# Conv means ahead of the first rotation, and the attention's modulation pair as direct TensorE products

## The chip, the cores and the metric

The program runs on one core of one Trainium2 chip. The metric is the device time of one launch, in microseconds (us); lower is better. The core has a matrix engine (TensorE, "PE" in the profile), a vector engine (VectorE, "DVE"), an engine for functions and copies (ScalarE, "ACT"), GpSimd ("POOL") and SyncE ("SP"), which here only issues DMA transfers. Each engine works through its own instructions in order; they wait for each other on semaphores. TensorE's clock has two levels here, 2.4 GHz (a granted clock of 1.00) and 1.2 GHz (0.50).

## The reference, cut to what matters

Two blocks are computed one after the other, three layers in all. The change is in the first layer, of this function:

```python
for l in range(DEPTH):
    sh1, sc1, g1, sh2, sc2, g2 = adaln(c, w_mod[l], b_mod[l])            # silu(c) @ w_mod + b_mod, split in 6
    csh1, csc1, cg1, csh2, csc2, cg2 = adaln(c_ctx, w_mod[l], b_mod[l])
    h = modulate(rms_norm(x, norm1_g[l]), sh1, sc1)
    hc = modulate(rms_norm(xc, norm1_g[l]), csh1, csc1)
    q, k, v, up, ca, cb = project_inputs(h, w_in[l], q_norm_g[l], k_norm_g[l])
    qc, kc, vc, upc, cac, cbc = project_inputs(hc, w_in[l], q_norm_g[l], k_norm_g[l])
    q = apply_rope(q, cos, sin)
    k = apply_rope(k, cos, sin)
    attn = diff_attn_post(diff_attention(q, k_all, v_all, lam), subln_g[l], lambda_init)
    pool_o = pool_mixer(up, pool_w[l], pool_scale[l])
    conv_o = conformer_conv(ca, cb, ...)       # depthwise conv of 31 taps, layer_norm over 256 channels, silu
    mix = jnp.concatenate([attn, pool_o, conv_o], axis=-1)
    x = x + g1 * jnp.einsum('blm,md->bld', mix, w_out[l])
...
```

The model has 1024 channels, 512 tokens and 256 context tokens; four heads, each with two score maps of 64 channels.

## The kernel before, in words

Tokens lie in the free dimension (512 + 256 in layer 0, `TOK` = 768), channels on the 128 partitions. Weights come in blocks of 256 columns. SP loads a block into `raw`, ACT copies it to a rounded high part (`w_hi`), GpSimd subtracts to get the low part (`w_lo`), and PE multiplies three times (high by high, high by low, low by high). In layer 0's input blocks 2 to 9 DVE makes the low part itself (`own_lo`), since GpSimd computes the pool windows there.

Layer 0 has ten input blocks. Blocks 0 to 3 give the inputs of convolution and pool, 4 to 7 give queries and keys (two tiles of 128 channels each), 8 and 9 give the values. Four output blocks follow the attention. Everything is written out by hand, engine by engine; no scheduler moves anything.

**Modulation pairs.** The columns of `w_mod` are taken 512 at a time, as a "pair" (l, p) of two rings of 256. SP loads a pair once the pair before it is saved (`load_pair`, semaphores `mod_saved` and `mod_landed`). DVE multiplies each of the eight row tiles by the condition's column and adds up, 16 steps for condition and context condition together (`pair_steps`, L2174, over `mod_w` and `mod_ctx`). PE then sums over the partitions by eight matmuls with a column of ones (`pair_sum`, L2494; in the trace a float32 matmul leaves two records, so 16), and DVE or ACT copies eight columns to `modc`. Pair (0,7), `PAIR_ATT`, has its 16 steps in two halves behind rotations 2 and 3, its sums in `second_root`, its copy on ACT (L2042); the first scores wait for that. Pair (0,6) belongs to block 7, pair (0,8) to the first output block.

**The queries and keys.** For tile pair j (blocks 4 to 7) ACT squares and copies, PE sums the squares by head (`head_sum`, L2634), ACT takes the root, DVE inverts it (`inverse`). For the rotation SP swaps odd and even channels by DMA (`load_swap`, semaphore `p_swap`); `rotate(j)` is three DVE instructions (L2263 to L2265). The swap of j = 2 and 3 waits until rotation j - 2 is done. For keys the root is spread by ACT (`spread_root`), turned by PE (`turn_root`, L2706) and multiplied in by DVE (`finish_k`, L2273).

**The convolution.** 62 taps on DVE leave `conv_acc`. PE sums over the channels (`conv_sums`, L2666, behind the first tile of block 7), DVE subtracts the mean (L2305, `c_yc`), ACT squares, PE sums again (`conv_square_sum`, L2686), ACT and DVE make the root (`c_root`), ACT spreads it, PE turns it (`conv_root_turned`, L691, behind tile 4 of block 8) and DVE multiplies (L2327, `c_yn`). In block 7 `head_sum` of keys waits for `c_yc`.

**GpSimd.** The pool windows start when the last step of pair (0,6) is done.

**The attention.** 24 units in layer 0, six to a head: four of 128 queries by 768 keys, then two small ones of 128 context queries by 256 context keys. PE makes the scores of unit u + 2, multiplies by v for unit u - 1 where a pair of units is complete, and turns unit u (`later`). PE's order between blocks 8, 9 and the attention is set by these dictionaries:

```python
between = {4: conv_root_turned} if b == 8 else {
    0: lambda: turn_root(4), 2: second_root, 3: first_score, 4: lambda: turn_root(6),
    5: lambda: turn_root(7)}
```

## Time and profile before

| | |
|---|---|
| three runs | 2577.93, 2583.73, 2584.11 us; median 2583.73 |
| the profiled execution | 2577.28 us, of which 2575.5 us from its first to its last instruction |
| busy shares | PE 95%, PE's weight loads 78%, DVE 52%, ACT 31%, POOL 34% |
| mean granted TensorE clock | 0.966 |
| chain that ended last | PE 86%, DVE 9%, ACT 3%, issue 1%, DMA 1% |
| DMA | 240.57 MB, mean 93 GB/s |

The chain follows the work that ended last back to its start, each step to what released it. A row of the timeline gives start and length of merged instructions of one line; in brackets stands how long the engine was idle before, and who ended that. Pages and rows are of one execution. Busy PE is not PE at its peak: at a clock of 0.50 it is busy twice as long for the same work.

### The profile page before, as it was taken

The page shows a single profiled execution, that of the slowest core. Times are in us where ns is not written, and L with a number is a line of the kernel's source. Part 1 is how long each engine was busy: PE and PEld are TensorE (multiplying, and loading weights), DVE is VectorE, ACT ScalarE, POOL GpSimd, SP SyncE. Part 2 cuts the span into 40 slices and gives each one's busy share as a digit, 9 for nine tenths or more (in the row PEclk, how much of TensorE's full clock was granted, in tenths as well). Part 3 has the DMA queues.
Part 4 walks back from the last instruction along what each step waited for, and adds up shares of the span by engine and source line. Part 5 has one row for each costly group of instructions (what it writes and reads, how often), then busy time and mean ns, then how long its engine had stood idle before and what let it go on. Part 6 is the DMA issues. An engine that isn't in the chain of part 4 may idle for free.

```text
span 2575.5 us, 30755 instructions
## 1 busy us (share of the span) xinstructions
PE 2445.3 (95%) x13017; PEld 2019.1 (78%) x13017; DVE 1337.2 (52%) x1709; ACT 798.5 (31%) x1088; POOL 884.9 (34%) x633
## 2 busy tenths in 40 slices
PE   7999899999999999899999999998999988999998
PEld 3888778788888888778777778877988557888886
DVE  2899766646444343695656655654562424211113
ACT  2222661311211111425732122235343443222222
POOL 2006002223333332365034445543453003454442
PEclk9898899899999999899999999998999999999999
DMA  8332203224334242232034546432113002233331
GB/s 265 95 104 83 66 1 111 70 87 143 99 113 132 82 131 82 65 107 75 1 98 131 149 146 175 151 115 66 50 35 114 17 1 65 70 95 98 90 98 58
DMA packets 309225, 240.57 MB, mean 93 GB/s; under 512 B 10692, under 2 KB 304831, under 8 KB 309087
## 3 DMA queue, kind: packets, MB, share of 16 engines
q1 hardware_dynamic: 308674, 238.47, 30.5%
q8 instruction: 103, 1.69, 0.3%
q14 instruction: 34, 0.28, 0.0%
q10 hardware_dynamic: 414, 0.13, 0.0%
HBM read 232.29 MB, written 2.10 MB: 91 GB/s over the span
## 4 chain that ended last, share of the span: by engine, by line
PE 86%; DVE 9%; ACT 3%; issue 1%; DMA 1%; POOL 0%; SPq 0%; DVEq 0%; ACTq 0%
PE ps L2542 62%; PE ps L1162 5%; DVE mod_w L2174 2%; PE ps L2577 2%; PE ps L946 2%; PE ps L684 2%; DVE mod_ctx L2174 1%; PE ps L733 1%; PE ps L1182 1%; PE ps L2457 1%; PE ps L2494 1%; PE ps L760 1%; DVE small L1050 1%; PE ps L908 1%; ACT probs L990 1%
## 5 line engine op out<-in xcount | busy, mean ns | idle before, releaser
L1680 POOL TENSOR_TENSOR w_lo<-raw,w_hi 128x512 fp32r<-128x512 f32 x518 | 757.2, 1492 | 1380.5 <-ACT w_hi L1788 1380.4
L2542 PE MATMUL ps<-h_hi,w_hi 128*128 128x512 f32 x1994 | 649.4, 372 | 25.2 <-DVE h_lo L2138 21.1
L2542 PE MATMUL ps<-h_lo,w_hi 128*128 128x512 f32 x1994 | 639.5, 367 | 0.0
L2542 PE MATMUL ps<-h_hi,w_lo 128*128 128x512 f32 x1994 | 638.9, 366 | 0.0
L1788 ACT ACTIVATE w_hi<-raw 128x2048 fp32r<-128x2048 f32 (+2 forms) x155 | 264.8, 1708 | 577.3 <-PE ps L2542 365.3
L2542 PEld LDWEIGHTS ps<-h_hi,w_hi 128*128 128x128 f32 x1994 | 340.4, 191 | 93.9 <-issue 23.1
L2542 PEld LDWEIGHTS ps<-h_hi,w_lo 128*128 128x128 f32 x1994 | 339.9, 190 | 67.1
L2542 PEld LDWEIGHTS ps<-h_lo,w_hi 128*128 128x128 f32 x1994 | 340.4, 190 | 65.9 <-issue 0.2
L2065 ACT ACTIVATE xg<-ps 128x512 f32<-128x512 f32 (+1 forms) x66 | 44.2, 670 | 679.4 <-PE ps L2542 492.6
L2174 DVE SCALAR_TENSOR_TENSOR mod_w<-mod_w,cond 128x512 f32<-128x512 f32 x224 | 242.0, 1080 | 3.4
L2542 PE MATMUL ps<-hid_hi,w_hi 128*128 128x512 f32 x704 | 231.7, 370 | 0.0
L2542 PE MATMUL ps<-hid_lo,w_hi 128*128 128x512 f32 x704 | 230.3, 368 | 0.0
L2542 PE MATMUL ps<-hid_hi,w_lo 128*128 128x512 f32 x704 | 230.3, 368 | 0.0
L2423 DVE TENSOR_TENSOR sq<-xg,ps 128x512 f32<-128x512 f32 (+1 forms) x66 | 51.1, 775 | 342.6 <-ACT xg L2065 342.5
L2201 DVE SCALAR_TENSOR_TENSOR x<-ps,modc,x 128x512 f32<-128x512 f32 (+1 forms) x160 | 100.6, 678 | 208.1 <-PE ps L2542 208.1
L2542 PEld LDWEIGHTS ps<-hid_hi,w_lo 128*128 128x128 f32 x704 | 120.4, 188 | 24.6
L2542 PEld LDWEIGHTS ps<-hid_lo,w_hi 128*128 128x128 f32 x704 | 120.5, 188 | 24.3
L2542 PEld LDWEIGHTS ps<-hid_hi,w_hi 128*128 128x128 f32 x704 | 120.5, 188 | 24.0
L2426 DVE TENSOR_TENSOR hid_lo<-sq,hid_hi 128x512 fp32r<-128x512 f32 (+1 forms) x66 | 90.2, 1367 | 85.8 <-ACT hid_hi L2068 85.8
L1087 DVE SCALAR_TENSOR_TENSOR conv_acc<-u_conv,col_b,conv_acc 128x783 f32<-128x783 f32 (+1 forms) x120 | 123.6, 1030 | 4.2
L2174 DVE SCALAR_TENSOR_TENSOR mod_ctx<-mod_w,cond,mod_ctx 128x512 f32<-128x512 f32 x112 | 108.3, 967 | 0.0
L1162 PE MATMUL ps<-h_hi,w_hi 128*128 128x512 f32 (+1 forms) x196 | 73.3, 374 | 0.9 <-POOL w_lo L1680 0.9
(380 smaller groups left out, 3225.8 us busy)
## 6 DMA issues: line engine op xcount, KB each, us to landing
mod_w<-in_w_mod SPq DMA_DIRECT2D x72, 1024.0 KB, 9.6
raw<-in_w_ffn_in SPq DMA_DIRECT2D x88, 512.0 KB, 5.3
raw<-in_w_in SPq DMA_DIRECT2D x54, 512.0 KB, 4.9
raw<-in_w_ffn_out SPq DMA_DIRECT2D x48, 384.0 KB, 3.8
raw<-in_w_out SPq DMA_DIRECT2D x24, 512.0 KB, 4.6
raw<-in_w_gate SPq DMA_DIRECT2D x22, 512.0 KB, 4.0
raw<-in_w_up SPq DMA_DIRECT2D x22, 512.0 KB, 5.4
raw<-in_w_down SPq DMA_DIRECT2D x24, 384.0 KB, 3.8
```

The source lines that it names most:

```text
L684: ins = pe.matmul(ps[:, at + j:at + j + 1], square[:, P * j:P * j + P], ones[:, 0:1], start=first and j == 0, stop=last, skip_group_check= ...
L946: ins = pe.matmul(ps[:, PV2_AT:PV2_AT + 256], values(us[u]["k0"] // P + k, us[u]["h"]), probs_t[:, k, 256 * (j % 2):256 * (j % 2) + 256], ...
L1087: ins = dve.scalar_tensor_tensor(acc, frm, w, acc, ALU.mult, ALU.add)
L1162: ins = pe.matmul(ps[:, at:at + tw], weight, v[:, k, t0:t0 + tw], start=(k == 0 and r == 0), stop=(k == KD - 1 and r == 2))
L1680: ins = pool.tensor_tensor(w_lo[:, s, at:end], raw[:, s, at:end], w_hi[:, s, at:end].bitcast(F32), ALU.subtract)
L1788: act.activation(w_hi[:, s, 0:floats], raw[:, s, 0:floats], ACT.Copy).then_inc(hi_ready, 1)
L2174: ins = dve.scalar_tensor_tensor(to, w, by, to if step >= chains else mod_bias[:, :, :], ALU.mult, ALU.add)
L2201: ins = dve.scalar_tensor_tensor(xt, ps[:, at:at + tw], modc[:, l % 2, chunk + 2 * b + t, c:c + 1], xt, ALU.mult, ALU.add)
L2423: dve.tensor_tensor(ffn_h[:, s, 0:T], ffn_sg[:, s, 0:T], ps[:, 2048 * s + 1024:2048 * s + 1024 + T], ALU.mult).then_inc(psum_free[s], 1)
L2426: dve.tensor_tensor(hid_lo[:, i, 0:T], ffn_h[:, s, 0:T], hid_hi[:, i, 0:T].bitcast(F32), ALU.subtract).then_inc(f_lo, 1)
L2542: ins = pe.matmul(ps[0:m, at:at + tw], weight(part, k, cols), v[:, held[k] if held else k, t0:t0 + tw], start=(at_k == 0 and j == 0 and no ...
L2577: ins = pe.matmul(ps[:, first + width * t:first + width * (t + 1)], v[:, k, rows], w[:, k, :], start=(k == 0 and j == 0), stop=(k == KD - ...
```

## The change

It has four parts, all in layer 0.

1. DVE subtracts the conv means after 4 steps of pair (0,6), ahead of rotation 0, where it had done 8 steps and rotation 0 first. The other 12 steps follow, then the low part of block 8, rotation 0, the low part of block 9, rotation 1.
2. Pair (0,7) leaves DVE. PE multiplies the loaded weights directly (weights as the stationary operand, the two condition columns as the moving one), a quarter of the pair at a time: eight matmuls of two columns and one for the bias, behind the scores of the two small units of heads 0 and 1. ACT copies two columns after that unit's exponentials; the score that reuses the place waits for the copy.
3. The old sums of this pair in `second_root`, its copy and the wait of the first score go.
4. The 16 steps of pair (0,8) stood behind the last low part of the mix. Six of them now stand behind the attention's last unit, five behind the low parts of the convolution, five at the old place. Its load waits, as before, for pair (0,7) to be saved, which is now after unit 11.

```diff
@@ -170,7 +170,7 @@
-        pair_ops.append(pair_ops[-1] + (2 * KD if pair_both(m) else KD))
+        pair_ops.append(pair_ops[-1] + (0 if m == PAIR_ATT else 2 * KD if pair_both(m) else KD))
@@ -886,6 +887,14 @@
+        def direct_tile(l, u):
+
+            h, place = u // 6, u % 6 - 4
+            return 2 * h + place if l == 0 and place >= 0 and h < 2 else None
+
+        def direct_at(u):
+            return 1536 * (u % 2) + 1024
@@ -899,6 +908,10 @@
                 if u >= 2:
                     pe.wait_ge(at_exp, comp_base[l] + 2 * u - 2)
+                    if direct_tile(l, u - 2) == 3:
+                        pe.wait_ge(mod_saved, pairs_saved(PAIR_ATT))
+                    elif direct_tile(l, u - 2) is not None:
+                        pe.wait_ge(att_saved, direct_tile(l, u - 2) + 1)
@@ -947,11 +960,18 @@
+            def direct(u):
+
+                d, to = direct_tile(l, u), ps[:, direct_at(u):direct_at(u) + 2]
+                ring, e = d // 2, d % 2
+                pe.wait_ge(mod_landed, 48 * (pair_at[PAIR_ATT] + 1))
+                for k in range(KD):
+                    pe.matmul(to, mod_w[:, ring, 256 * k + P * e:256 * k + P * e + P], cond[:, 0, k, :], start=(k == 0), stop=False)
+                pe.matmul(to, mod_bias[0:1, ring, P * e:P * e + P], ones[0:1, 0:2], start=False, stop=True).then_inc(att_pair, 1)
+
             def first_score():
                 pe.wait_ge(psum_free[0], base_out[l] // 2)
-                if l == 0:
-                    pe.wait_ge(mod_saved, pairs_saved(PAIR_ATT))
                 score(0)
@@ -969,6 +989,8 @@
                 if u + 2 < len(us):
                     score(u + 2)
+                    if direct_tile(l, u + 2) is not None:
+                        direct(u + 2)
                 times_v(u - 1)
@@ -1010,6 +1032,16 @@
+            def direct_out(u):
+
+                d = direct_tile(l, u)
+                act.wait_ge(att_pair, d + 1)
+                ins = act.activation(modc[:, 0, 4 * PAIR_ATT[1] + d, :], ps[:, direct_at(u):direct_at(u) + 2], ACT.Copy)
+                if d == 3:
+                    ins.then_inc(mod_saved, 2)
+                else:
+                    ins.then_inc(att_saved, 1)
@@ -1030,6 +1062,8 @@
                 if u + 1 < len(us):
                     exponentials(u + 1)
+                    if direct_tile(l, u + 1) is not None:
+                        direct_out(u + 1)
                 save(u - 1)
...
@@ -2292,12 +2319,11 @@
                     if l == 0:
-                        pair_steps((0, 6), 0, KD)
-                    inverse(0)
-                    rotate(0)
-                    if l:
-                        inverse(1)
-                        rotate(1)
+                        pair_steps((0, 6), 0, KD // 2)
+                    else:
+                        for j in range(2):
+                            inverse(j)
+                            rotate(j)
                     dve.wait_ge(c_sum, l + 1)
@@ -2306,11 +2332,13 @@
                     if l == 0:
-                        pair_steps((0, 6), KD, 2 * KD)
+                        pair_steps((0, 6), KD // 2, 2 * KD)
                         own_lo(8)
+                        inverse(0)
+                        rotate(0)
+                        own_lo(9)
                         inverse(1)
                         rotate(1)
-                        own_lo(9)
                     for j in range(2, 4):
@@ -2318,16 +2346,12 @@
-                            if l == 0:
-                                pair_steps(PAIR_ATT, 0, KD)
...
-                    if l == 0:
-                        pair_steps(PAIR_ATT, KD, 2 * KD)
@@ -2354,6 +2378,9 @@
+                    first_out_pair = pair_in_block.get(base_out[l])
+                    if first_out_pair:
+                        pair_steps(first_out_pair, 0, 6)
                     head_args(0, HEADS - 1, 1, 0)
@@ -2363,6 +2390,8 @@
+                    if first_out_pair:
+                        pair_steps(first_out_pair, 6, 11)
                     head_inverse(0, HEADS - 1, 1)
@@ -2397,7 +2426,7 @@
-                        pair_all(pair_in_block[n])
+                        pair_steps(first_out_pair, 11, 2 * KD)
```

On DVE, in block 7 of layer 0, a step of pair (0,6), the inversion and rotation 0 stood ahead of the centring (`conv_acc<-ps,conv_acc`) before:

```order
L2174 SCALAR_TENSOR_TENSOR mod_ctx<-mod_w,cond,mod_ctx 128x512 [waits mod_mul]
L2174 SCALAR_TENSOR_TENSOR mod_w<-mod_w,cond 128x2x256 [waits mod_mul]
L2257 RECIPROCAL qk_root<-qk_root 128x24 [waits p_std]
L2263 TENSOR_TENSOR qk_swap<-qk_swap,rot 128x1024 [waits p_swap0]
L2264 TENSOR_TENSOR qk<-qk,rot 128x2x512
L2265 TENSOR_TENSOR qk<-qk,qk_swap 128x2x512 [waits dve_step]
L2305 SCALAR_TENSOR_TENSOR conv_acc<-ps,conv_acc 128x512 [waits c_sum]
L2305 SCALAR_TENSOR_TENSOR conv_acc<-ps,conv_acc 128x256
```

The same place with the change; the steps before and behind the centring are those of pair (0,6):

```order
L2205 SCALAR_TENSOR_TENSOR mod_ctx<-mod_w,cond,mod_ctx 128x512 [waits mod_mul]
L2205 SCALAR_TENSOR_TENSOR mod_w<-mod_w,cond 128x2x256 [waits mod_mul]
L2331 SCALAR_TENSOR_TENSOR conv_acc<-ps,conv_acc 128x512 [waits c_sum]
L2331 SCALAR_TENSOR_TENSOR conv_acc<-ps,conv_acc 128x256
L2331 SCALAR_TENSOR_TENSOR conv_acc<-ps,conv_acc 128x512
L2331 SCALAR_TENSOR_TENSOR conv_acc<-ps,conv_acc 128x256
L2205 SCALAR_TENSOR_TENSOR mod_ctx<-mod_w,cond,mod_ctx 128x512 [waits mod_mul]
```

The centring stands four steps, the inversion and three rotation instructions earlier. Rotation 0 comes behind the low part of block 8, and rotation 1 behind the low part of block 9:

```order
L2307 TENSOR_TENSOR w_lo<-raw,w_hi 128x2048 [waits hi_ready]
L2284 RECIPROCAL qk_root<-qk_root 128x24 [waits p_std]
L2290 TENSOR_TENSOR qk_swap<-qk_swap,rot 128x1024 [waits p_swap0]
L2291 TENSOR_TENSOR qk<-qk,rot 128x2x512
L2292 TENSOR_TENSOR qk<-qk,qk_swap 128x2x512 [waits dve_step]
L2307 TENSOR_TENSOR w_lo<-raw,w_hi 128x2048 [waits hi_ready]
L2284 RECIPROCAL qk_root<-qk_root 128x24 [waits p_std]
L2290 TENSOR_TENSOR qk_swap<-qk_swap,rot 128x1024 [waits p_swap1]
```

On PE, in the attention, the scores of unit 4 (the first small unit of head 0, `swap_hi` and `qk_lo`) were followed by the value product of units 0 and 1 and the turn of unit 2:

```order
L908 MATMUL ps<-swap_hi 128x256 [waits at_exp]
L908 MATMUL ps<-swap_hi 128x256
L908 MATMUL ps<-swap_hi,qk_lo 128x256 x2
L908 MATMUL ps<-qk_lo,swap_hi 128x256 x2
L946 MATMUL ps<-probs_t,v_nat 128x256 [waits at_copied]
L946 MATMUL ps<-probs_t,v_nat 128x256 x5
L935 MATMUL ps<-const,probs 128x128 [waits at_copied,at_a]
```

With the change:

```order
L921 MATMUL ps<-swap_hi 128x256 [waits at_exp]
L921 MATMUL ps<-swap_hi 128x256
L921 MATMUL ps<-swap_hi,qk_lo 128x256 x2
L921 MATMUL ps<-qk_lo,swap_hi 128x256 x2
L969 MATMUL ps<-cond,mod_w 128x2 [waits mod_landed]
L969 MATMUL ps<-cond,mod_w 128x2 x7
L970 MATMUL ps<-const,mod_bias 128x2
L959 MATMUL ps<-probs_t,v_nat 128x256 [waits at_copied]
L959 MATMUL ps<-probs_t,v_nat 128x256 x5
L948 MATMUL ps<-const,probs 128x128 [waits at_copied,at_a]
```

Nine narrow matmuls stand between scores and value product. The same is added at units 5, 10 and 11.

On DVE, behind the last unit, the sum of squares of three heads (`sums_eps<-sums`) was followed directly by the wait for PE's sums:

```order
L1074 SCALAR_TENSOR_TENSOR sums_eps<-sums 128x24
L2348 TENSOR_TENSOR n_root<-sums_eps,ps 128x18 [waits m_ss,dve_step]
L2363 TENSOR_TENSOR h_lo<-conv_acc,h_hi 128x512 [waits m_hi,at_t]
L2363 TENSOR_TENSOR h_lo<-conv_acc,h_hi 128x256
L2363 TENSOR_TENSOR h_lo<-conv_acc,h_hi 128x512 [waits m_hi]
L2363 TENSOR_TENSOR h_lo<-conv_acc,h_hi 128x256
L2355 RECIPROCAL n_root<-n_root 128x18 [waits m_std]
```

With the change, steps of pair (0,8) stand in both places; the first row is the last of six:

```order
L2205 SCALAR_TENSOR_TENSOR mod_w<-mod_w,cond 128x2x256 [waits mod_mul]
L2372 TENSOR_TENSOR n_root<-sums_eps,ps 128x18 [waits m_ss]
L2390 TENSOR_TENSOR h_lo<-conv_acc,h_hi 128x512 [waits m_hi,at_t]
L2390 TENSOR_TENSOR h_lo<-conv_acc,h_hi 128x256
L2390 TENSOR_TENSOR h_lo<-conv_acc,h_hi 128x512 [waits m_hi]
L2390 TENSOR_TENSOR h_lo<-conv_acc,h_hi 128x256
L2205 SCALAR_TENSOR_TENSOR mod_ctx<-mod_w,cond,mod_ctx 128x512 [waits mod_mul]
L2205 SCALAR_TENSOR_TENSOR mod_w<-mod_w,cond 128x2x256 [waits mod_mul]
L2205 SCALAR_TENSOR_TENSOR mod_ctx<-mod_w,cond,mod_ctx 128x512 [waits mod_mul]
L2205 SCALAR_TENSOR_TENSOR mod_w<-mod_w,cond 128x2x256 [waits mod_mul]
L2205 SCALAR_TENSOR_TENSOR mod_ctx<-mod_w,cond,mod_ctx 128x512 [waits mod_mul]
L2379 RECIPROCAL n_root<-n_root 128x18 [waits m_std]
```

Six steps moved ahead of `n_root<-sums_eps`, five between the conv's low parts and the inversion of `n_root`; the last five stay behind the head products.

## Rows read from the trace of the kernel before

**Rows 1.** The waits of PE at 196 to 410 us (us in total, times, longest).

```profile
PE ps L908 <- ACT probs L990: 6.6, 9, 2.7
PE ps L2494 <- DVE mod_w L2174: 5.2, 1, 5.2
...
PE ps L2706 <- DVE qk L2273: 4.7, 1, 4.7
...
PE ps L2634 <- issue: 1.3, 1, 1.3
```

**Rows 2.** Six stretches (length, busy us by engine, granted clock, DMA share, GB/s).

```profile
core 0: us, PE busy (x) PEld busy (x) DVE busy (x) ACT busy (x) POOL busy (x), PEclk, DMA share, GB/s
203.60:207.10 3.50, 2.16 (x17) 2.03 (x17) 3.50 (x8) 1.87 (x4) 0.00 (x0) 1.00 0.40 150
207.10:227.60 20.50, 20.50 (x93) 19.92 (x92) 15.58 (x13) 4.93 (x7) 16.36 (x14) 0.50 0.24 78
258.90:268.60 9.70, 9.70 (x46) 9.70 (x46) 2.69 (x3) 2.54 (x4) 0.00 (x0) 0.50 0.31 106
311.00:322.00 11.00, 10.43 (x67) 8.23 (x66) 9.20 (x20) 7.45 (x22) 0.00 (x0) 1.00 0.00 0
398.70:405.10 6.40, 6.39 (x25) 6.00 (x26) 2.30 (x5) 2.28 (x2) 0.79 (x1) 0.50 0.21 57
1158.00:1165.00 7.00, 7.00 (x56) 6.65 (x55) 0.00 (x0) 0.39 (x1) 6.39 (x9) 1.00 0.02 4
```

**Rows 3.** The chain of waits at 160 to 270 us (start, us, what).

```profile
164.51 1.68 PE ps L2494 x16
...
219.42 3.22 PE ps L2494 x16
...
263.62 5.22 PE ps L2577 x24
```

**Rows 4.** The timeline of DVE (start, us, what, [idle before]).

```profile
193.81 0.74 DVE L2174 SCALAR_TENSOR_TENSOR mod_ctx<-mod_w,cond,mod_bias 128x512 f32<-128x512 f32 x1
...
199.45 1.16 DVE L2263 TENSOR_TENSOR qk_swap<-qk_swap,rot 128x1024 f32<-128x1024 f32 x1
...
202.92 1.95 DVE L2305 SCALAR_TENSOR_TENSOR conv_acc<-ps,conv_acc 128x512 f32<-128x512 f32 x4
204.78 0.74 DVE L2174 SCALAR_TENSOR_TENSOR mod_ctx<-mod_w,cond,mod_ctx 128x512 f32<-128x512 f32 x1
205.44 0.74 DVE L2174 SCALAR_TENSOR_TENSOR mod_w<-mod_w,cond 128x512 f32<-128x512 f32 x1
...
212.49 2.33 DVE L2263 TENSOR_TENSOR qk_swap<-qk_swap,rot 128x1024 f32<-128x1024 f32 x1
...
224.61 2.29 DVE L2280 TENSOR_TENSOR w_lo<-raw,w_hi 128x2048 fp32r<-128x2048 f32 x1 [4.88 <-ACT w_hi L1788]
...
245.42 1.94 DVE L2327 TENSOR_TENSOR conv_acc<-conv_acc,ps 128x512 f32<-128x512 f32 x4
```

**Rows 5.** The timeline of PE, two turns and the conv sums.

```profile
195.60 2.75 PE L2666 MATMUL ps<-conv_acc,const 128*128 128x512 f32 x8
...
241.42 0.82 PE L691 MATMUL ps<-const,v_nat 128*128 128x128 f32 x6
...
247.74 0.81 PE L2706 MATMUL ps<-const,qk_sq 128*128 128x128 f32 x6
```

**Rows 6.** The timeline of GpSimd, where its pool windows start.

```profile
210.24 3.50 POOL L1736 TENSOR_TENSOR u_conv<-u_pool 128x799 f32<-128x799 f32 x1 [147.01 <-DVE mod_w L2174]
```

**Rows 7.** The timeline of SP, the swap for rotation 3.

```profile
227.82 1.26 SPq L563 DMA_DIRECT2D qk_swap<-qk  x2
```

**Rows 8.** The timeline of DVE behind the last unit.

```profile
365.86 0.17 DVE L2348 TENSOR_TENSOR n_root<-sums_eps,ps 128x18 f32<-128x18 f32 x1 [5.64 <-PE ps L684]
...
371.79 0.27 DVE L2355 RECIPROCAL n_root<-n_root 128x18 f32<-128x18 f32 x1 [3.86 <-ACT n_root L1953]
```

**Rows 9.** The timeline of ACT, the copy of the attention's pair.

```profile
263.71 0.18 ACT L2042 ACTIVATE modc<-ps 128x8 f32<-128x8 f32 x1 [2.36 <-PE ps L2494]
```

More of the change, by code:

```diff
@@ L373, in program @@
         mod_sum, mod_copied, mod_cols = sem("mod_sum"), sem("mod_copied"), sem("mod_cols")
-        mod_saved, mod_mul, bias_clear, att_pair = sem("mod_saved"), sem("mod_mul"), sem("bias_clear"), sem("att_pair")
+        mod_saved, mod_mul, bias_clear, att_pair, att_saved = (sem("mod_saved"), sem("mod_mul"), sem("bias_clear"), sem("att_pair"),
+                                                               sem("att_saved"))
         w_landed = [sem("w_landed0"), sem("w_landed1")]
@@ L431, in mod_part @@
             return mod_w[:, ring, 0:256]
-        IN_MOD_AT, ATT_MOD_AT, MOD_AT = 3840, 0, 1792
+        IN_MOD_AT, MOD_AT = 3840, 1792
         def pair_columns(n):
@@ L2039, in _ @@
                             spread_root(7)
-                            if l == 0:
-                                act.wait_ge(att_pair, 1)
-                                pair_out(lambda to, frm: act.activation(to, frm, ACT.Copy), PAIR_ATT, ATT_MOD_AT)
                     next_hi(base_in[l] + 9)
@@ L2175, in pair_steps @@
                     ins.then_inc(mod_mul, 1)
-            def pair_all(m):
-                pair_steps(m, 0, 2 * KD if pair_both(m) else KD)
             def pair_halves(n):
@@ L2328, in _ @@
                         ins.then_inc(c_yn, 1)
-                    if l == 0:
-                        pair_steps(PAIR_ATT, KD, 2 * KD)
                     finish_k(4)
@@ L2739, in second_root @@
                         turn_root(5)
-                        if l == 0:
-                            pe.wait_ge(psum_free[0], base_out[0] // 2)
-                            pair_sum(PAIR_ATT, ATT_MOD_AT).then_inc(att_pair, 1)
                     for b in range(10):
```

## The prediction

> **What bounds the kernel now.** I read the page first. PE is busy for 95% of the span and carries 86% of the chain that ended last, so an edit on DVE can only pay where PE waits for it, or where PE runs at the lower of its clock levels. The waits of PE in the edited stretch (196 to 410 us) come next [rows 1]. Three of them are edited: 5.2 us for the last modulation step before the first output block's pair sums, 4.7 us for a key tile (DVE queued behind steps of the attention's pair), and 1.3 us at the key sums of block 7. The profile names no engine for that one ("issue"). It ends when DVE has centred the convolution, which the code waits for there (c_yc). The third view is the granted clock [rows 2]. It falls to 0.50 of 2.4 GHz, that is 1.2 GHz, in or behind each of these three places: 207.1 to 227.6, about 258.9 to 268.6, and 398.7 to 405.1 us. Half speed costs more here than the waits themselves. It is not idling alone that lowers it: at 203.6 to 207.1 PE was still busy for 2.16 of 3.5 us. What it did were sums of one or two columns. In layer 1 the same kinds of sums at 1158 to 1165 us, without idle time and with fewer of them, kept 1.00.
>
> **Centring ahead of the first rotation.** DVE starts the steps of pair (0,6) at 193.81; steps start 0.66 apart [rows 4]. Four of them end at 196.5. The conv sums on PE end at 198.35 [rows 5], so DVE now idles 1.9 us, and centres (1.95) until 200.3. Before, this ended at 204.9. PE reaches its wait at 203.6 (204.97 less 1.34), so the 1.34 us go. I take it that the clock still falls near 207.1, because the narrow sums are still there. Then 1.3 us more of the work is done at full clock, worth another 1.3 us, and block 8 starts 2.7 us earlier at half clock, so the rise comes earlier too, worth half of 2.7. Term: 1.34 + 1.3 + 1.35 = **4.0 us**. Bounds: 1.3 (no help from the clock) and 1.34 plus half of 20.5 us, 11.6 (no fall at all).
>
> **What that does to DVE.** After 200.3 come 12 steps (7.95), until 208.3. GpSimd waits for the last one: it started at 210.24 before [rows 6], 208.4 now. The low part of block 8 (2.2) ends at 210.6. Rotation 0 follows, now beside GpSimd. Alone it took from 199.45 to 202.92, 3.5 us, its first instruction 1.16; rotation 1 beside GpSimd took from 212.49 to 219.73 (224.61 less the 4.88 idle), 7.2 us, its first instruction 2.33 [rows 4]. So I take about 7.4 us instead of 3.5, until 218.0. The low part of block 9 waits for ACT, behind the end of block 7 (219.42 + 3.22 = 222.64 before [rows 3], about 220 now): it ran at 224.61 after 4.88 idle us [rows 4], and will end at about 224. Rotation 1 is now behind it. That delays a transfer: SP issued the swap of keys for rotation 3 at 227.82 [rows 7], and it needs rotation 1, so it now goes at 230 to 231. Rotation 1 and 2 at 5.8 us each (between 3.5 and 7.4, partly beside GpSimd) end at 229.9 and 235.7, the spread root is there at 236.6, and PE comes for it at 241.42 [rows 5] less 4.0 = 237.4. Rotation 3 starts at 237.0 without the eight steps that stood ahead of it, and ends at 241 to 242.5; the product with the turned root takes 1.94 [rows 4], until 243 to 244.5. PE wants that at 247.74 [rows 5] less 4.0 = 243.7. So the chain on DVE just holds, at 0 to 0.8 us. I charge 0 and keep this as a rival.
>
> The Trainium skill, SBUF — State Buffer, section Who interferes with whom, bears on this: a VectorE instruction with two SBUF inputs and a GpSimd instruction that reads SBUF exclude each other for a whole instruction, and the one issued first wins. By that rule moving rotation 0 behind GpSimd's start speaks against the change; the trace agrees, with 1.16 against 2.33 us [rows 4].
>
> **The attention's pair off DVE.** Sixteen steps go (10.6 us uncontended). The eight behind the turned root kept the key tile until 257.8. Now the key tile follows at once. PE asked for it at 258.9 - 4.7 = 254.2 and now asks at 250.2, the product ended by 244.5, and the tile needs about 1 us: the 4.7 us are gone. With them goes the fall of the clock: 258.9 to 268.6 held 9.7 us of PE work at 0.50 [rows 2]: a turn, pair sums of 3.2 us (the same sixteen records at 219.42 took 3.22 [rows 3]), and a value tile of 5.22 [rows 3]. The sums go; the other 6.5 us take about 3.4 at full clock. Term: **4.7 + 6.3 = 11.0 us**, bounds 4.7 + 1.7 (the clock falls anyway) and 11.4.
>
> **The direct products.** Each of four has eight products with two columns and one for the bias, two passes each: 18 loads and matmuls. Sixteen such took 1.68 us at 164.51 at full clock and 3.22 at half [rows 3], so one direct product costs 1.9 us (half clock 3.6). They stand where PE has no room: at 311 to 322 us, the small units of head 1, it was busy 10.43 of 11 us [rows 2]. So 7.6, less 0.57 in each of two heads, and the scores now wait for four small copies on ACT (0.18 us for eight columns [rows 9], two columns now, so at most that), which adds about 0.5 together. Term: **-7.0 us**. Bounds: -14.9 (all at half clock, nothing hidden) and 0 (all in waits, 6.6 us of PE's waiting for exponentials [rows 1]).
>
> The Trainium skill, TensorE: Matmul & The Clock Gate, section LDWEIGHTS, says that a load's time follows its columns and not its rows. By it the bias product, with one row, costs as much as the others; no row here has such a load of 128 columns. Would it be free, the term would be about 0.8 us smaller.
>
> **The output pair.** Its transfer now waits for unit 11 of the attention's 24 and is wanted behind the last one; a transfer of this pair was a matter of about 10 us on the page (median 9.6). Six steps (4.0 us) go into DVE's 5.64 idle us ahead of 365.86, five (3.3) into the 3.86 ahead of 371.79 [rows 8]. Five remain at the end. Sixteen steps (10.6) ended at 398.7, so they began at 388.1; five end at 391.4, and PE is through its products at 398.7 - 5.2 = 393.5. So the 5.2 us go, and PE's 6.4 us at 0.50 [rows 2] shrink by 3.2. Term: **8.4 us**; bounds 5.2 and 8.4.
>
> **Sum.** 4.0 + 11.0 - 7.0 + 8.4 = 16.4 us. Behind 410 us PE has no new cause to wait. The profiled execution took 2577.28 us (span 2575.5 and 1.8 around it); it stands 6.5 us under the median of 2583.73. So 2560.9 on the profiled execution, and **2567 us** for the median.
>
> **Rivals.**
> *DVE's rotations take over (17%).* If rotations 1 and 2 cost the full 7.4 us, the spread root comes at 240, PE idles 2.4 us, rotation 3 and the product end at 249 to 250, and PE idles 3 more. A fall of the clock as at 258.9 follows and costs 4.9. Of 16.4, 6.1 are left: 2578. For it: the lock above, and the swap delayed by 3. Against it: rotation 3 ran nearly alone before, and eight steps fewer compete with GpSimd.
> *Only the waits go, the clock falls at other places (12%).* 1.3 + 4.7 + 5.2 + 1.7 (pair sums) - 7.0 = 5.9: 2578. For it: 1158 and 207 show how close the two cases are.
> *No fall behind 207 at all (13%).* The row of layer 1 speaks for it [rows 2], the narrower sums of layer 0 and the pair sums behind them against it. DVE's chain then limits PE, 3 us better than the forecast, but no more: 19.4 us, 2564.
> *Slower (5%).* The direct products pull the clock down in the small units of heads 0 and 1 and it stays down over the 11 us stretch. They cost 14.9 then, and the work of both stretches doubles, 10.43 us each [rows 2]: 21. That gives 23.4 - 14.9 - 21 = -12.5, 2596. It decides from 8.5 us of such slowed work on. For it: narrow sums stood where the clock fell at 207. Against it: wide score and value products stand between the direct ones.
> The forecast itself has 53%.
>
> **How the numbers follow.** A measurement of this kernel tells 0.3% (7.75 us) from no change, so faster means under 2576. The forecast, the third rival and a third of the first two give 0.76. Slower has 0.05 and the rest, 0.19, is the same. The range takes the no-fall case and, with the measured spread of 6 us between runs, 9 us below it, 2555, and reaches above to the first rivals, 2579.
>
> **What would show it.** Right: no wait of PE at the key sums of block 7, for the key tile and for the pair of the first output block; clock 1.00 between block 9 and the first scores; the first scores near 254 instead of 268.8; four groups of 18 narrow matmuls of 1.9 us and attention longer by 7. Wrong: a wait of PE at the turned conv root or behind it, narrow matmuls at twice the time, or a DVE step that PE still waits for near 385.

## The result, and the profile after

The changed kernel takes 2562.56 us (median of 4 runs, 2561.44 to 2567.31) against 2583.92 of the kernel before beside it (4 runs): the medians differ by 21.4 us. The ratio over all runs is 0.9934, 95% interval 0.9917 to 0.995, which is 17 us (13 to 21). On a second chip (5 runs against 18) it was 0.9925 (0.9913 to 0.9938). The profiled execution took 2561.44 us, its span is 2559.7. That is 15.8 us under before's profiled execution, which stood 6.6 us under its own median.

The waits of PE at 196 to 410 us (us in total, times, longest). They answer to [rows 1]: the waits for `mod_w`, for the key tile and the one called issue are gone; the rest belongs to the attention.

```profile
PE ps L921 <- ACT probs L1012: 6.1, 7, 2.7
PE ps L948 <- DVE probs L1095: 3.3, 3, 1.8
PE ps L959 <- ACT probs_t L1023: 1.4, 2, 0.9
PE ps L921 <- ACT v_nat L2040: 0.9, 1, 0.9
```

Six stretches after (length, then busy us of PE, PEld, DVE, ACT, POOL, the granted clock, DMA share, GB/s), to read beside [rows 2]:

```profile
202.70:208.80 6.10, 6.10 (x50) 5.83 (x50) 6.10 (x8) 0.00 (x0) 1.39 (x1) 1.00 0.00 0
208.80:219.10 10.30, 10.30 (x47) 10.01 (x47) 8.80 (x6) 2.70 (x4) 9.99 (x5) 0.50 0.09 32
250.20:266.80 16.60, 12.64 (x111) 11.61 (x112) 10.64 (x14) 11.28 (x16) 7.28 (x6) 1.00 0.18 63
266.80:304.40 37.60, 34.76 (x198) 28.88 (x196) 27.95 (x48) 23.84 (x55) 0.00 (x0) 0.77 0.09 29
304.40:348.40 44.00, 39.00 (x267) 30.51 (x265) 32.65 (x60) 33.13 (x82) 0.00 (x0) 1.00 0.16 49
387.70:402.00 14.30, 14.30 (x82) 12.39 (x83) 9.13 (x14) 3.50 (x3) 5.77 (x4) 1.00 0.75 222
```

The clock still falls behind the narrow sums, but PE is busy throughout before it and the fall is half as long: 208.8 to 219.1 instead of 207.1 to 227.6. The one at 259 and the one at 399 are gone. The first scores start at 250.2, where the forecast had them near 254. New is the fourth row: early in the attention the mean clock is 0.77. The same 37.6 us of before:

```profile
285.60:323.20 37.60, 32.58 (x203) 25.61 (x200) 32.08 (x59) 29.12 (x70) 0.00 (x0) 0.91 0.26 85
```

DVE and GpSimd after (start, us, what, [idle before, releaser]), to read beside [rows 4] and [rows 6]:

```profile
197.43 1.95 DVE L2331 SCALAR_TENSOR_TENSOR conv_acc<-ps,conv_acc 128x512 f32<-128x512 f32 x4 [0.23 <-PE ps L2695]
...
209.66 2.32 DVE L2290 TENSOR_TENSOR qk_swap<-qk_swap,rot 128x1024 f32<-128x1024 f32 x1
...
218.35 2.42 DVE L2307 TENSOR_TENSOR w_lo<-raw,w_hi 128x2048 fp32r<-128x2048 f32 x1 [1.46 <-ACT w_hi L1822]
...
220.91 1.16 DVE L2290 TENSOR_TENSOR qk_swap<-qk_swap,rot 128x1024 f32<-128x1024 f32 x1
...
232.03 1.51 DVE L2290 TENSOR_TENSOR qk_swap<-qk_swap,rot 128x1024 f32<-128x1024 f32 x1 [1.25 <-DMA qk_swap<-qk]
...
237.61 1.94 DVE L2353 TENSOR_TENSOR conv_acc<-conv_acc,ps 128x512 f32<-128x512 f32 x4
```

```profile
207.41 3.50 POOL L1770 TENSOR_TENSOR u_conv<-u_pool 128x799 f32<-128x799 f32 x1 [143.61 <-DVE mod_w L2205]
...
218.71 9.78 POOL L1783 TENSOR_TENSOR u_conv<-u_conv,const 64x8 f32<-64x8 f32 x8
...
239.14 2.14 POOL L1783 TENSOR_TENSOR u_conv<-u_conv,const 64x8 f32<-64x8 f32 x8
```

Rotation 0 ran beside GpSimd at twice its time, as forecast; rotations 1 and 2 (220.9 to 228.1) ran at the short one (1.16) and made up for it. GpSimd worked beside them too, but on eight small additions, and there it was GpSimd that waited: the eight took 9.78 us, and the same eight later, with DVE idle for most of the time, 2.14. The product with the turned conv root ended at 239.5, ahead of PE.

PE after, the first direct product and its bias product, and the pair sums of the first output block:

```profile
270.25 1.95 PE L969 MATMUL ps<-cond,mod_w 128*128 128x2 f32 x16
272.13 0.38 PE L970 MATMUL ps<-const,mod_bias 1*128 1x2 f32 x2
272.44 0.92 PE L959 MATMUL ps<-probs_t,v_nat 128*128 128x256 f32 x3
...
385.85 0.28 PE L2523 MATMUL ps<-const,mod_w 128*128 128x1 f32 x2
```

From start to start the sixteen take 1.88 us, the two of the bias 0.31: 2.19 us for a direct product, not 1.9. All four direct products ran at full clock here.

**Stages.** All kernels of this study run the same code outside three stages, so I read each profiled execution in them: A, from the first record of the conv sums to that of the first scores; B, from there to the end of the last scores; C, from there to the first pair sum of the third output block. D is what follows to the end, and the 193 to 196 us ahead of A are in no column. The ratios come from all runs, the stages from the one execution that was profiled. From the PE timelines, in us:

```
                                     A      B      C   A+B+C     D      ratio of times (95%)
before                             73.2   87.5   81.3   241.9  2138.0
after                              55.6   98.3   73.1   227.0  2138.2   0.9934 (0.9917-0.9950)
after, second chip                 57.1   98.5   73.1   228.8  2135.2   0.9925 (0.9913-0.9938)
means early alone                  73.3   86.8   82.7   242.8  2146.0   0.9995 (0.9985-1.0005)
attention pair alone               64.7   98.4   82.6   245.8  2139.6   1.0015 (1.0006-1.0024)
split alone                        72.9   86.4   71.5   230.8  2141.0   0.9952 (0.9939-0.9965)
means + split                      74.2   86.8   71.2   232.1  2142.3   0.9971 (0.9960-0.9982)
means + attention pair             57.1   99.1   82.6   238.9  2142.5   1.0001 (0.9992-1.0009)
after, no direct products          58.7   88.1   72.9   219.7  2142.6   0.9926 (0.9915-0.9938)
after, pair on GpSimd              57.2  100.1   71.5   228.8  2137.8   0.9951 (0.9936-0.9966)
after, pair steps in gaps          59.8   92.6   71.2   223.6  2145.5   0.9924 (0.9907-0.9942)
after, gaps refined                57.3   91.1   71.5   219.9  2138.0   0.9891 (0.9870-0.9913)
after, direct in heads 1 and 2     57.4   98.5   69.8   225.7  2141.0   0.9959 (0.9945-0.9972)
after, rotation 0 first            58.7   99.1   73.0   230.7  2141.8   0.9943 (0.9924-0.9962)
```

### The profile page after: what moved, and what is told of

Read it like the earlier page. It is cut to its first block, busy times and chain, and to the rows that moved or that the text cites. A ratio compares the mean times of both kernels' runs of the same rounds, so it can differ in the third digit from the quotient of the medians.

```text
span 2559.7 us, 30855 instructions
## 1 busy us (share of the span) xinstructions
PE 2441.3 (95%) x13073; PEld 2016.5 (79%) x13073; DVE 1320.2 (52%) x1693; ACT 798.8 (31%) x1091; POOL 884.1 (35%) x633
## 3 DMA queue, kind: packets, MB, share of 16 engines
q1 hardware_dynamic: 308674, 238.47, 30.7%
## 4 chain that ended last, share of the span: by engine, by line
PE 87%; DVE 8%; ACT 3%; issue 1%; POOL 0%; DMA 0%; DVEq 0%; SPq 0%; ACTq 0%
PE ps L2571 62%; PE ps L1196 5%; PE ps L2606 3%; PE ps L959 2%; PE ps L734 1%; DVE mod_w L2205 1%; PE ps L1216 1%; PE ps L2486 1%; DVE mod_ctx L2205 1%; PE ps L685 1%; PE ps L761 1%; PE ps L921 1%; DVE small L1084 1%; PE ps L2523 1%; DVE xg L2182 1%
## 5 line engine op out<-in xcount | busy, mean ns | idle before, releaser
L2205 DVE SCALAR_TENSOR_TENSOR mod_w<-mod_w,cond 128x512 f32<-128x512 f32 x217 | 234.5, 1081 | 3.4
L2205 DVE SCALAR_TENSOR_TENSOR mod_ctx<-mod_w,cond,mod_ctx 128x512 f32<-128x512 f32 x105 | 99.8, 951 | 0.0
L1084 DVE TENSOR_REDUCE small<-ps 128x2 f32<-128x1536 f32 (+1 forms) x40 | 61.6, 1541 | 28.4 <-PE ps L921 28.3
```

The source lines that it names most:

```text
L1084: link(dve.tensor_reduce(tops, ps[:, at:at + 2 * apart].rearrange("p (c k) -> p c k", c=2)[:, :, 0:v["nk"]], AXX, ALU.max, negate=True))
L2205: ins = dve.scalar_tensor_tensor(to, w, by, to if step >= chains else mod_bias[:, :, :], ALU.mult, ALU.add)
```

## The experiments

Each was timed in five rounds beside before on one chip.

**1. Conv means early, alone.**

```diff
-                        pair_steps((0, 6), 0, KD)
-                    inverse(0)
-                    rotate(0)
...
+                        pair_steps((0, 6), 0, KD // 2)
...
-                        pair_steps((0, 6), KD, 2 * KD)
+                        pair_steps((0, 6), KD // 2, 2 * KD)
                         own_lo(8)
+                        inverse(0)
+                        rotate(0)
+                        own_lo(9)
                         inverse(1)
                         rotate(1)
-                        own_lo(9)
```

> The kernel before with the first part alone: conv means centred after four steps of pair (0,6), rotation 0 behind the low part of block 8. Theory (the wait and the clock both count, and they pass on): PE does not wait at the key sums of block 7, block 8 starts 6 us earlier than before, and the time falls by 4 to 6 us. Rival (the key tile absorbs it: the eight attention-pair steps behind the turned conv root stay, and they are bound to DVE's chain, not to PE's): block 8 starts earlier, PE waits longer than 4.7 us for the key tile, and of the gain 0 to 2 us are left.

Nothing was gained, and the rival says why. PE's waits (us in total, times, longest) and the DVE timeline of this kernel:

```profile
PE ps L2495 <- DVE mod_w L2174: 5.2, 1, 5.2
PE ps L2707 <- DVE qk L2273: 4.7, 1, 4.7
PE ps L2707 <- DVE conv_acc L2328: 4.1, 1, 4.1
```

```profile
230.55 0.76 DVE L2174 SCALAR_TENSOR_TENSOR mod_ctx<-mod_w,cond,mod_bias 128x512 f32<-128x512 f32 x1 [2.29 <-DMA mod_bias<-in_b_mod]
...
245.78 1.42 DVE L2174 SCALAR_TENSOR_TENSOR mod_ctx<-mod_w,cond,mod_ctx 128x512 f32<-128x512 f32 x1
247.12 1.77 DVE L2174 SCALAR_TENSOR_TENSOR mod_w<-mod_w,cond 128x512 f32<-128x512 f32 x1
...
257.72 0.94 DVE L2273 TENSOR_TENSOR qk<-qk,ps 128x768 f32<-128x768 f32 x1
```

The pair sums of (0,6) start 6.2 us earlier than before (212.98, 219.22; 1.0 of it lies ahead of stage A), but PE then waits 4.1 us for the conv product and 4.7 for the key tile. DVE sets both: its first step of the attention's pair waits for a transfer, and the last eight take 11.9 us beside GpSimd, 1.1 to 1.8 each instead of 0.74. The key tile comes at 257.7, where it came before.

**2. The attention's pair as direct products, alone.** The change without its edits to the DVE order of pair (0,6), the centring and the output pair.

> The kernel before with the attention's pair as direct products alone; DVE's order of pair (0,6), of the centring and of the output pair stays. Theory by the forecast's terms: 11.0 - 7.0 = 4.0 us faster than before. Rival, by what the two traces show (attention 10.8 us longer, first scores 11.5 earlier than the shift already gained): 0 to 1.5 us, that is nothing that can be told from before. In both the wait for the key tile (4.7) goes.

4 us slower (1.5 to 6), which neither the theory nor the rival had. The first scores come 8.5 us sooner behind the conv sums (A), and the attention is 10.9 longer (B). PE still idles 2.8 us at the key sums of block 7, and the clock was at 0.50 from 204.5 to 228.4. C is 1.3 longer and D 1.6.

**3. The output pair split, alone.**

```diff
+                        pair_steps(first_out_pair, 0, 6)
                     head_args(0, HEADS - 1, 1, 0)
...
+                        pair_steps(first_out_pair, 6, 11)
                     head_inverse(0, HEADS - 1, 1)
...
-                        pair_all(pair_in_block[n])
+                        pair_steps(first_out_pair, 11, 2 * KD)
```

> The kernel before with the steps of the first output block's pair split alone (six ahead of the head sums, five ahead of the reciprocal, five at the end). Theory: PE's wait of 5.2 us ahead of that pair's sums goes and the clock stays up over them and the products behind: 8.4 us faster. Rival (only the wait goes, or the steps delay the last head sums): 3 to 5.2 us.

0.9952, that is 12 us, more than either. Stage C is 9.8 us shorter. Over all kernels C has a mean of 82.3 us without the split (four) and 71.9 with it (ten): 10.4. The forecast's 8.4 left out that the fall of the clock was 10.2 us long in three of the four without the split (392 to 409), not before's 6.8. The rest goes with a second fall, behind the last scores (it starts at 350 to 365 us). It is 6.8 us long in all four without the split, and in the ten with it 6.8, 3.4 or absent, where C is 72.9 to 73.1, 71.2 to 71.5 and 69.8. Before and after both have 6.8 there; whether the split shortens it is not shown.

**4. Without the direct products.** The eight products of each group are left out, the bias product stays.

> The kernel after without the eight products of each direct group: only the bias product of each stays, so the attention pair's modulation is only its bias (this part of the computation is left out). Order, waits and copies stay. The four groups lose 4 x 1.88 = 7.5 us of PE work at full clock. Theory (the products pull the clock down as well: after has five falls of 3.4 us between 266 and 305, before one of 6.8): one fall is left, 7.5 less 1.5 hidden plus 5 of clock, so 9 to 11 us faster than after. Rival (the falls come from PE's idle time and the turns, since the first, at 266.85, is ahead of the first direct product at 270.3): the falls stay and 5 to 7 us are gained.

B is 88.1 instead of 98.3: 10.2 back for 7.5 of removed work. The stretches (columns as above):

```profile
254.00:271.50 17.50, 13.11 (x115) 11.87 (x114) 11.63 (x15) 12.28 (x18) 4.97 (x4) 1.00 0.20 62
271.50:308.50 37.00, 32.81 (x200) 26.34 (x202) 31.26 (x57) 27.95 (x71) 0.00 (x0) 0.91 0.14 47
```

One fall of 6.8 us is left (clock 0.91, as before). The fall begins without direct products too, but with them it comes back four times, 17.1 us at 0.50 within B instead of 6.8: the theory holds. The ratio, 0.9926, does not show the 7 us by which A+B+C is shorter than after's: in the profiled execution, which is the median one, stage D took 4.4 us more.

**5. After again, on the chip of experiments 6 to 8.**

> The kernel after once more, beside the three that follow. It is 0.9934 of before in the result. Its profile shows whether the times of the stages repeat: first scores 18.6 us earlier than before, attention (first scores to the head sums behind it) 103 us against 92.3.

A, B and C repeat within 1.5 us each, D within 3.0. In B the clock was at 0.50 for 17.1 us again, in three falls instead of five, and the first direct product ran inside one: it took 4.0 us.

**6. Means early and split, attention's pair on DVE.**

> Conv means early and the output pair split, the attention's pair still on DVE. Theory (the early means alone are taken back by DVE's chain, where eight attention-pair steps stand ahead of the key tile): the same as the split alone, 12.4 us faster than before, ratio 0.995 to 0.996. Rival (the terms of the forecast add): 4 to 6 us more, ratio 0.993 to 0.9935, as fast as after, and the attention pair's move is worth nothing.

0.9971, 7.5 us: not more than the split alone, by time even less. A is 74.2: again nothing from the early means.

**7. Means early and direct products, no split.**

> Conv means early and the attention's pair as direct products, the output pair as before. Theory (the two need each other: alone they gave 0 and 4 us slower): 9 us faster than before, ratio 0.9965, since after is 21.4 faster and the split alone is worth 12.4. Rival (additive): 4 us slower than before, ratio 1.0015, and the split would then be worth more in after than alone.

The time missed what I expected (9 us) and came out as before's. The 9 us mixed a difference of medians (21.4) with one from a ratio (12.4); by ratios alone it is 5. The stages are in between: A 16.1 shorter, B 11.6 longer, C 1.3 longer, together 3.0 faster, and D took 4.5 more in the profiled execution. A is the finding: the early means gain 0 without the direct products (73.2 to 73.3) and 7.6 with them (64.7 to 57.1); the direct products alone gain 8.5 there, and 16.2 with early means.

**8. The attention's pair on GpSimd.** 32 multiplications and additions on GpSimd behind the low part of output block 1, sums on PE once, in unit 16.

```diff
+                    for k in range(1, KD):
+                        w = mod_w[:, :, 256 * k:256 * k + 256]
+                        link(pool.tensor_tensor(part_of, w, by(k, 1), ALU.mult))
+                        link(pool.tensor_tensor(mod_ctx[:, :, :], mod_ctx[:, :, :], part_of, ALU.add))
+                        link(pool.tensor_tensor(w, w, by(k, 0), ALU.mult))
+                        link(pool.tensor_tensor(sums, sums, w, ALU.add))
```

> The kernel after with the attention pair's weighted sum made by GpSimd in its idle time behind the low part of the second output block (from 266 us, 32 operations of about 1.1 us, 35 us), and PE's pair sums (16 records, 1.7 us) once, in unit 16, in place of four direct products (8.8 us). Theory: PE's work falls by 7 us; GpSimd's reads slow DVE's weighted difference (1.02 us, about ten of them beside GpSimd) to about 2, which is on the loop of the attention, so 3 us of it come back; 3 to 7 us faster than after. Rival (contention eats it): DVE's two-input operations at twice the time keep PE waiting for probs, the attention is as long as after's 103 us or longer, no gain.

The rival. PE has 7 us less to do, yet B is 100.1. The timelines of both engines, and the wait that grew from 3.3 us:

```profile
298.10 1.86 POOL L1815 TENSOR_TENSOR mod_ctx<-mod_ctx,mod_bias 128x512 f32<-128x512 f32 x1
```

```profile
301.51 1.73 DVE L1089 SCALAR_TENSOR_TENSOR probs<-probs,small 128x768 f32<-128x768 f32 x1
...
316.43 1.02 DVE L1089 SCALAR_TENSOR_TENSOR probs<-probs,small 128x768 f32<-128x768 f32 x1
```

```profile
PE ps L945 <- DVE probs L1089: 9.6, 8, 3.3
```

Until GpSimd ends, at 314, seven weighted differences take 1.30 to 1.73 us instead of 1.02, and GpSimd's own additions 1.27 to 1.9. The Trainium skill, SBUF — State Buffer, section Who interferes with whom, says that such instructions of the two exclude each other; these rows agree. PE's waits for DVE grew from 3.3 us in total to 9.6, which eats 6.3 of the 7 us. The clock took more: within B it was at 0.50 for 23.9 us, 17.1 in after. Whether the longer waits brought that on is not shown. A+B+C is what it was in after on this chip (228.8), the ratio, 0.9951, is worse.

**9. The pair's steps in DVE's gaps.** Back on DVE, 16 steps in the gaps around the key tiles and ahead of the maximum of unit 5, sums on PE once (unit 10).

```diff
                     finish_k(4)
+                    att(0, 4)
                     split_heads_lo(dve, l, 0)
                     finish_k(5)
+                    att(4, 6)
...
             top(0)
+            att(6, 8)
             k_tile(6)
+            att(8, 11)
             k_tile(7)
...
+                if u == 3:
+                    att(11, 16)
```

> The kernel after with the attention's pair back on DVE, its 16 steps cut into the gaps that after's trace shows behind the turned conv root: four ahead of the low half of head 0 (3.7 us idle there), two ahead of the first maximum (1.8), two and three around the last key tiles (1.6 and 2.5), five ahead of the maximum of unit 5; PE makes the pair sums once (16 records, 1.7 us) in unit 10 in place of four direct products (8.8). Theory: first scores stay 16 to 18 us earlier than before, the attention takes 94 to 97 us instead of 103, so 6 to 8 us faster than after, ratio to before 0.990 to 0.9905. Rival (the gaps are not free: GpSimd's windows run until 246 and its split until 266, a step beside them takes 1.9 instead of 0.75 us, and the key tiles come late): first scores or first units late by 5 or more, no faster than after.

B is 92.6, 5.7 under after's. The first scores came at 255.5, 13.3 us earlier than before and not 16 to 18. Of the 4.2 us by which A is over after's, 3.4 are clock (6.8 us more at 0.50, an estimate at half), and 0.9 is a new wait of PE for the low half of head 0. There the rival is right, though at a smaller size: the first gap was not free.

```profile
250.72 1.76 DVE L2203 SCALAR_TENSOR_TENSOR mod_w<-mod_w,cond 128x512 f32<-128x512 f32 x1
252.40 2.92 DVE L887 TENSOR_TENSOR qk_lo<-qk,swap_hi 128x768 fp32r<-128x768 f32 x2
```

A+B+C is 3.4 under after's. The ratio, 0.9924 (0.9907 to 0.9942), is after's and misses the 0.990 to 0.9905 expected. Stage D took 7 us more in the profiled execution, but that was the slowest of six, 7.4 us above their median, so it does not explain the ratio.

**10. Direct products in heads 1 and 2.**

```diff
-            return 2 * h + place if l == 0 and place >= 0 and h < 2 else None
+            return 2 * (h - 1) + place if l == 0 and place >= 0 and 0 < h < 3 else None
```

> The kernel after with the four direct products in the small units of heads 1 and 2 instead of 0 and 1. Theory (the cost is 8.8 us of work on an engine without room, place matters little): attention 102 to 104 us, same time as after. Rival (the cost is the falls of the clock that the direct products prolong at the start of the attention, 267 to 304 us; behind 310 it has been at 1.00 throughout): attention 98 to 100 us, 3 to 5 us faster than after.

B is 98.5: the place matters little, as the theory said. The clock at the start of the attention had one fall of 3.4 us (266.8), and later ones came with the products (287.3, 294.2, 318.0), 17.1 us in all, as in after. The time is not what the theory said: 0.9959 (0.9945 to 0.9972) is slower than after on its second chip (0.9913 to 0.9938), if not clearly than its first result (0.9917 to 0.995). A+B+C, 225.7, does not show it, since the profiled execution was the fastest of nine; the cause stays open.

**11. Rotation 0 ahead of the steps.** `inverse(0)` and `rotate(0)` directly behind the centring.

> The kernel after with rotation 0 directly behind the centring, ahead of the twelve steps of pair (0,6), so that it runs before GpSimd starts (3.5 us instead of 7.3), and GpSimd starts 3.5 us later. Theory (DVE idles 1.46 us ahead of the low part of block 9 and 2.24 ahead of the spread root, rotation order is not on the path): the same as after within 1.5 us, conv root turned at 234 to 235. Rival (the lock of DVE and GpSimd is on the path): turned root or key tile 2 to 4 us earlier or, with GpSimd's work moved onto rotations 1 and 2, later.

Rotation 0 took 3.5 us instead of 7.2, and DVE then idled 7.4 us for ACT instead of 1.5. A is 58.7, 3.1 over after's, but as in the kernel without direct products, whose early clock was the same (17.1 us at 0.50 instead of 10.2): rotation 0 is not on the path. The ratio, 0.9943 (0.9924 to 0.9962), can't be told from after's.

**12. The gaps refined.** 2, 2, 2 and 3 steps around the key tiles, 3 ahead of the maximum of unit 5, 1, 1 and 2 ahead of those of units 11 to 13, sums in unit 16. Against experiment 9:

```diff
-                    att(0, 4)
+                    att(0, 2)
...
-                if u == 3:
-                    att(11, 16)
+                if u in (3, 9, 10, 11):
+                    att(*{3: (9, 12), 9: (12, 13), 10: (13, 14), 11: (14, 16)}[u])
```

> As the version with the pair steps in gaps, with a finer cut after its trace: there four steps beside GpSimd's windows took 1.0 to 1.8 us each and kept the low half of head 0 until 252.4, and five stood ahead of the maximum of unit 5. Now two, two, two and three steps around the key tiles, three ahead of the maximum of unit 5, one, one and two ahead of those of units 11, 12 and 13, where DVE idles 0.4, 0.5 and 1.3 us in the kernel without direct products; PE's pair sums in unit 16. Theory: scores of the attention (first start to last end) 89 to 91 us against 98.3 in after and 92.6 with the coarser cut, 6 to 9 us faster than after, ratio to before 0.989 to 0.991. Rival (what is gained in this stretch is given back by where the clock falls behind it, as the coarser cut's median showed: stage 5.7 us shorter, total the same): ratio 0.992 to 0.994.

2551.24 us (2550.63 to 2554.27) against 2580.33: ratio 0.9891 (0.987 to 0.9913), 28 us faster than before and the fastest kernel here, on four runs of a chip that after did not run on. Stretches of the attention and a later gap with its step:

```profile
251.80:269.90 18.10, 13.67 (x118) 12.40 (x118) 16.61 (x21) 12.71 (x18) 7.35 (x6) 1.00 0.21 67
269.90:306.00 36.10, 31.58 (x191) 24.42 (x191) 34.34 (x64) 27.49 (x67) 0.00 (x0) 0.91 0.08 26
```

```profile
299.33 0.75 DVE L2203 SCALAR_TENSOR_TENSOR mod_ctx<-mod_w,cond,mod_ctx 128x512 f32<-128x512 f32 x1
300.00 0.68 DVE L1078 TENSOR_REDUCE small<-ps 128x2 f32<-128x512 f32 x1
```

B is 91.1, 7.2 under after's and 3.6 over before's; C is 71.5. The clock of the second stretch is back at 0.91. Here the whole 7.1 us of A+B+C show in the time of the profiled executions (2554.27 against 2561.44); by the ratios the kernel gains 9 to 11 us on after.

## Why the prediction was right, step by step

**The sum.** Forecast 16.4 us on the profiled execution; it fell by 15.8, of which A+B+C hold 14.9 and the start ahead of A 1.0. The medians fell by 21.4, since before's profiled execution was a fast one of its kind. The median forecast, 2567, was 4.4 too high. That 15.8 came so near 16.4 is in part luck: A gained 2.6 us more than forecast, and the direct products cost 3.8 more.

**Means and attention pair, 4.0 + 11.0.** The three waits went, and A is 17.6 shorter (16.1 on the second chip). The sum came 1 to 3 us short, and the two terms were not separate ones, which the forecast took them for: the means alone are worth 0 (experiment 1), the pair alone 8.5 (2), both 16 (7). If half of the time at 0.50 is taken off each (an estimate), A is 57.8 us before, 59.7 with the means alone, 52.7 with the pair alone, and 50.1 to 50.6 with both, except in experiment 9 (51.3). So waits and work give 7 to 8 us of the 17.6, and the clock, at 0.50 for 10.2 us of A instead of 30.7, the other 10. The forecast's own step holds the reason: PE "asked for it at 258.9 - 4.7 = 254.2 and now asks at 250.2" only gains because the key tile no longer hangs on eight steps of DVE. Two sizes were off, in opposite ways. The shift of block 8 was 5.3 us (6.3 with the 1.0 ahead of A) instead of 2.7. The wait gave 1.3; the other 4.0 are clock, since PE's work ahead of block 8 ran at 0.50 for 7.4 us (208.8 to 216.2) instead of 15.5 (207.1 to 222.6). The whole fall became half as long (10.3 us; 13.7 on the second chip). And rotations 1 and 2 cost 3.5 us each, not 5.8, because the small GpSimd instructions beside them waited and hardly delayed DVE, so the first rival (DVE's rotations take over) had nothing to stand on; swap 3 was late, by 1.25 us, and that was covered. Experiment 11 shows that even 3.7 us more or less at rotation 0 change nothing.

**Direct products, 7.0.** This is the term that was mis-sized: 10.8 in this pair of traces, 10.9 to 11.6 in the others. Of the missing 3.8 us, 1.2 is their own price, 2.19 us each instead of 1.9: the bias product's records cost 0.155 each against 0.118 of the others. In the records one by one, those of a run stand 0.112 apart, and the step to the one-row product and the step back take 0.18 each. The Trainium skill, TensorE: Matmul & The Clock Gate, section LDWEIGHTS, has the load time follow the columns and not the rows; the trace agrees, with 0.181 to 0.184 us for a load of one row and 0.186 to 0.192 for one of 128. The larger part is the clock, which the forecast put at full speed: mean 0.77 over 37.6 us against 0.91, in B 17.1 us at 0.50 instead of 6.8, worth 5.1 (an estimate, at half). Together with 8.8 us of work that is 13.9; 3.1 of it were hidden, more than the forecast had, as PE's waits within B fell from 13.3 to 11.1. The "half clock 3.6" of its range came for none of the four products in this trace and for one on the second chip; what ran slowly was the work between them. The forecast had taken PE's time from the busiest stretch of before and had not looked at the clock at the start of the attention, where one fall was already in the trace. Removing the products gives all but 0.6 of it back (4), moving them does not (10).

**Output pair, 8.4.** In this pair of traces 8.2; over all kernels 10.4 (3). The steps ran in the gaps named: the last five ended at 383.7, PE's products at 385.8, without a wait.

**Rivals.** The second (only the waits go) and the fourth (slower) did not come; what the fourth feared did in part, more falls of the clock among the direct products, but at 5 us and not at 36. The third (no fall behind 207) did not come in any kernel here.

**What stays open.** Stage D is the same code in all fourteen executions and took 2135 to 2146 us. The clock differs there. The same place in the first experiment's kernel, in before and in after:

```profile
1090.00:1110.00 20.00, 16.83 (x61) 13.09 (x60) 19.43 (x18) 3.15 (x4) 13.41 (x8) 0.83 0.40 134
```

```profile
1090.00:1110.00 20.00, 16.85 (x73) 13.27 (x72) 19.43 (x17) 4.79 (x4) 13.47 (x8) 1.00 0.45 137
```

```profile
1086.00:1106.00 20.00, 20.00 (x97) 16.55 (x96) 19.32 (x21) 4.65 (x4) 8.22 (x5) 1.00 0.41 132
```

The seven executions with a fall there took 2142.9 on average, the seven without 2138.5. Over all fourteen the clock was at 0.50 for 99 to 120 us of stage D, and the stage was the longer the more there was of it, by about 0.44 us for one (a line through the fourteen). Why it falls more in one execution than in another these runs don't settle, but no edit is needed for it: before alone took 2571.8 to 2582.2 us in 23 executions on one chip, with mean clocks from 0.968 to 0.964. So one profiled execution does not tell what a median will be. By the ratios, after on the second chip and experiment 12 gained 6 us more than A+B+C says, experiment 10 gained 6 less, and 4, 6 and 7 gained 2 to 3 less.

## What to carry to other kernels

Don't add up the worth of edits that clear the same path one behind the other: find which engine's chain sets the next meeting point, since an edit ahead of it is worth nothing until that chain is shorter. Work taken from a vector engine to a full TensorE costs its whole duration and the clock that its narrow matmuls pull down (10.8 us for 8.8 of work); first look for gaps of one or two steps on the engine that had it, and leave those out that lie beside GpSimd. And where edits are worth a few us, compare the edited stretches of the traces beside the medians, and note how long the clock was low in each, since the unchanged rest moved by up to 11.

## What the hardware showed unexpectedly

- A weighted sum on GpSimd in its idle time cost PE as much as it saved: DVE's two-input instruction grew from 1.02 to as much as 1.73 us (8). Beside GpSimd's pool windows a modulation step grew from 0.74 to as much as 2.00 (1).
- How much DVE loses depends on what GpSimd runs: beside additions of 128x797 a rotation's first instruction took 2.32 us, beside additions of 64x8 it took 1.16, and those grew from 0.20 to 1.06 to 1.21 us each.
- The clock at 2.4 GHz fell to 1.2 at 208.8 us although PE had been busy for all of the 6.1 us before, in narrow sums between wide products.
- Two records with one row and two columns took 0.31 us, more than two of 128 rows (0.235), although the weight load took the same time.
- Identical code behind the edits varied by 11 us in 2140 with how long the clock was at 1.2 GHz.
